# Index scores moved from the attention phase into the last slots of the projections

## The reference, cut to what matters

```python
h = split_columns(x @ w_in)                  # all projections of the mixer
q_idx = apply_rope(q_idx.reshape(B, S, 8, 32), cos_i, sin_i)
k_idx = apply_rope(k_idx, cos_i, sin_i)      # one key of 32 for 8 query heads
rel = relu(einsum('bqhd,bsd->bqhs', qi, k_idx))
score = einsum('bqh,bqhs->bqs', wi, rel)     # 8 heads, weighted by token features
score = where(k_pos <= q_pos, score, -1e30)
_, idx = top_k(score, 128)
```

## Time and profile before

| | |
|---|---|
| median of 3 runs | 3699.91 us (3674.93, 3700.03, 3699.91) |
| the profiled execution | 3671.68 us, of which the span is 3669.9 us |
| granted TensorE clock, mean of the span | 0.964 |
| PE busy / PEld / DVE / ACT | 94% / 75% / 46% / 39% |
| projections, layer 0 (from the first product to the last) | 402.2 to 544.4 us |
| index scores, layer 0 | 553.9 to 571.1 us |
| attention units, layer 0 | to 728.1 us |

### The profile page before, as it was taken

One profiled execution on the slowest core, in us unless ns is written; L12 is line 12 of the kernel. 1 busy time (PEld: TensorE's weight loads), 2 busy tenths in 40 slices (PEclk: granted clock), 3 DMA queues, 4 the chain that ended last, 5 costly groups with the idle time before them and its releaser, 6 DMA issues. The chain is left out here.

```text
span 3669.9 us, 43503 instructions
## 1 busy us (share of the span) xinstructions
PE 3457.0 (94%) x15978; PEld 2748.0 (75%) x15978; DVE 1674.2 (46%) x2929; ACT 1424.3 (39%) x2341; POOL 77.5 (2%) x52
## 2 busy tenths in 40 slices
PE   7999989999999999999998999979999899889998
PEld 5888667677888788777776788757777677768886
DVE  3333448635333433334773533346655437343333
ACT  4332325454332433242545433235544427333321
POOL 0001000010001000100000100100000000000000
PEclk9999998989999999999898999989999999999999
DMA  3332330012332233233000233211211122223331
GB/s 135 97 105 93 103 87 1 1 35 80 97 108 87 70 97 104 95 96 99 12 1 19 80 97 104 95 45 58 70 65 65 59 92 91 85 69 97 97 108 65
DMA packets 81376, 281.21 MB, mean 77 GB/s; under 512 B 14400, under 2 KB 15936, under 8 KB 80704
## 3 DMA queue, kind: packets, MB, share of 16 engines
q1 hardware_dynamic: 81216, 279.13, 23.7%
HBM read 269.12 MB, written 2.10 MB: 74 GB/s over the span
## 5 line engine op out<-in xcount | busy, mean ns | idle before, releaser
L315 DVE TENSOR_TENSOR wlo<-raw,whi 128x1024 fp32r<-128x1024 f32 (+3 forms) x464 | 609.1, 1313 | 1037.6 <-ACT whi L311 1037.4
L343 PE MATMUL ps<-xh,whi 128*128 128x512 f32 x2320 | 912.8, 393 | 16.2 <-DVE xl L2441 6.3
L344 PE MATMUL ps<-xl,whi 128*128 128x512 f32 x2320 | 906.0, 391 | 0.0
L345 PE MATMUL ps<-xh,wlo 128*128 128x512 f32 x2320 | 905.2, 390 | 0.0
L311 ACT ACTIVATE whi<-raw 128x1024 fp32r<-128x1024 f32 (+3 forms) x464 | 515.3, 1111 | 655.8 <-PE ps L345 612.4
L343 PEld LDWEIGHTS ps<-xh,whi 128*128 128x128 f32 x2320 | 437.8, 189 | 117.4 <-issue 24.7
L344 PEld LDWEIGHTS ps<-xl,whi 128*128 128x128 f32 x2320 | 437.8, 189 | 91.5 <-issue 1.7
L345 PEld LDWEIGHTS ps<-xh,wlo 128*128 128x128 f32 x2320 | 437.5, 189 | 91.8
L343 PE MATMUL ps<-ffn_hh,whi 128*128 128x512 f32 x880 | 346.4, 394 | 11.1 <-DVE ffn_hl L747 11.1
L344 PE MATMUL ps<-ffn_hl,whi 128*128 128x512 f32 x880 | 344.6, 392 | 0.0
L345 PE MATMUL ps<-ffn_hh,wlo 128*128 128x512 f32 x880 | 344.2, 391 | 0.0
(11 more groups left out here) (368 smaller groups left out, 4317.7 us busy)
## 6 DMA issues: line engine op xcount, KB each, us to landing
raw<-in_ffn_up SPq DMA_DIRECT2D x216, 512.0 KB, 3.5
raw<-in_ffn_down SPq DMA_DIRECT2D x80, 704.0 KB, 4.0
raw<-in_ssm_in SPq DMA_DIRECT2D x44, 512.0 KB, 3.5
raw<-in_mix_in SPq DMA_DIRECT2D x32, 512.0 KB, 4.0
raw<-in_lru_in SPq DMA_DIRECT2D x20, 512.0 KB, 3.7
raw<-in_mix_out SPq DMA_DIRECT2D x16, 512.0 KB, 3.5
raw<-in_ssm_out SPq DMA_DIRECT2D x16, 512.0 KB, 3.4
raw<-in_lru_out SPq DMA_DIRECT2D x8, 640.0 KB, 3.8
```

The source lines that it names most:

```text
L315: dve.tensor_tensor(self.core.wlo[:, u % HALF, 0:width], self.core.raw[:, u, 0:width], self.core.whi[:, u % HALF, 0:width].bitcast(F32), A ...
L343: pe.matmul(out, c.whi[:, h, w], xh[:, k0 + k], start=first and k == 0, stop=False)
L344: pe.matmul(out, c.whi[:, h, w], xl[:, k0 + k], start=False, stop=False)
L345: mm = pe.matmul(out, c.wlo[:, h, w], xh[:, k0 + k], start=False, stop=last and k == nk - 1)
```

## The change

- Feature slots are reordered: the index features (`iq`) become slots 5 and 6, the compressed keys slot 4. The token block moves to slots 12 to 15 and into banks 0 to 3. The features of the fourth attention kind (`sq`, `sk`) come last, slots 16 to 19 (`stick_features`).
- The splits and the 24 index scores leave `mixer_attention`. Splits are done on ACT and DVE at slots 9 to 13. The scores go into the last four slots: behind each of the first six groups of 3 product matmuls one index score, six a slot, in PSUM banks 4 to 7. Relu, accumulation and masking follow on ACT and DVE inside the projections.
- The side products stand behind slots 3, 5, 6, 7, 13 and 14, and ACT evacuates each of them at the same slot number as PE computes it.
- SP issues the load of `cmp_w1` before slot 4 instead of behind `x_done`, and the copies of queries and keys earlier or later with their slots. Token copies (L1113) come at slot 15, the sigmoids at the end.

```diff
-    feat = [at[n] for n in "cq ckv dk krope ik nq kc vc ks kw dq iq sq sk".split()]
+    feat = [at[n] for n in "cq ckv dk krope ik kc vc iq nq ks kw dq sq sk".split()]
...
-STORED = (CQ, CQ + 1, CKV, KROPE, NSAQ, NSAQ + 1, KCMP, KSLC, DSAQ, DSAQ + 1, IDXQ, IDXQ + 1, SBQ, SBQ + 1, SBK, SBK + 1)
+STORED = (CQ, CQ + 1, CKV, KROPE, KCMP, IDXQ, IDXQ + 1, NSAQ, NSAQ + 1, KSLC, DSAQ, DSAQ + 1, SBQ, SBQ + 1, SBK, SBK + 1)
+TOK_AT = 12
...
+    rels = [(b, h) for h in range(IDXH) for b in range(1, QB)]
+    per_slot = len(rels) // (slots - TOK_AT - NTOK)
...
+                sp.dma_start(c1[:], d["cmp1"][l].rearrange("p (a j n) -> p a j n", a=2, j=16)).then_inc(ph["c1_in"], 16)
                 load(4)
...
-                beside = {3: lat_sums, 6: queries, 9: keys, 10: values, 12: compress, 14: compressed}
...
+                def stick_features(n):
+
+                    pe.wait_ge(ph["tok_out"], n - TOK_AT - NTOK + 1)
+                    pe.wait_ge(ph["lo_done"], n + 1)
+                    out, s = c.ps[:, n % 4], n % HALF
+                    some = list(rels_of(n))
+                    for t in range(DT):
+                        w = slice(t * P, (t + 1) * P)
+                        pe.matmul(out, c.whi[:, s, w], c.xh[:, t], start=t == 0, stop=False)
+                        pe.matmul(out, c.whi[:, s, w], c.xl[:, t], start=False, stop=False)
+                        mm = pe.matmul(out, c.wlo[:, s, w], c.xh[:, t], start=False, stop=t == DT - 1)
+                        if t == DT - 1:
+                            mm.then_inc(ph["slot_used"], 1)
+                        elif t < len(some):
+                            index_scores(some[t])
+
+                beside = {3: lat_sums, 5: queries, 6: keys, 7: values, 13: compress, 14: compressed}
...
-                beside = {2: squares, 4: roots, 7: queries, 10: keys, 11: values, 13: gelus, 15: compressed}
+                beside = {2: squares, 3: roots, 5: queries, 6: keys, 7: values, 9: lambda: index_hi(0), 10: lambda: index_hi(1),
+                          11: lambda: index_hi(2), 13: gelus, 14: compressed, slots - 1: gates}
...
                 for n in range(slots):
+                    relus(n)
                     act.wait_ge(ph["slot_used"], n + 1)
...
+                    if n == TOK_AT + NTOK - 1:
+                        token_out()
+                    if n == TOK_AT + NTOK:
+                        dve.wait_ge(ph["tok_out"], QB)
+                    accumulate(n)
                     ph.lo(dve, n // 4, n % 4, width(n + 2), last=n >= slots - 4)
-                    if n == 5:
+                    if n == 4:
                         latents()
                     if n - 2 in ROTATED:
                         rope(order.index(n - 2))
...
+                    if n in (9, 10, 11, 14):
+                        rope_query((9, 10, 11, 14).index(n))
+                    if n in (10, 11, 13):
+                        index_lo((10, 11, 13).index(n))
+                    if n == 12:
                         windows()
...
-                pe.wait_ge(ph["lo_done"], n_index)
-                for i in range(len(rels)):
-                    index_scores(i)
-
-                pe.wait_ge(ph["relu_done"], len(rels))
```

More of the change, by code:

```diff
@@ L837, in mixer_front, with rels_of @@
     c2 = c.at("cmp_w2", [64, 192], F32, W + 87 * KB)
-    c1 = c.at("cmp_w1", [P, 2, 16, HD], F32, W + 88 * KB)
+    c1 = c.at("cmp_w1", [P, 2, 16, HD], F32, W + 2 * SBQ * KB)
     ukv = c.at("ukv_w", [P, 2, HEADS * HD], F32, W + 98 * KB)
-    hid = c.at("cmp_hid", [64, 2, NCMP], F32, W + 96 * KB)
+    hid = c.at("cmp_hid", [64, 2, NCMP], F32, W + 87 * KB + 768)
+    rel = c.at("idx_rel", [P, 4, SEQ], F32, W + 54 * KB)
     slots = NFEAT + NTOK
     order = list(ROTATED)
-    width = lambda n: D if n < NFEAT else TOKW
+    in_tok = lambda n: TOK_AT <= n < TOK_AT + NTOK
+    feature = lambda n: n if n < TOK_AT else n - NTOK
+    width = lambda n: TOKW if in_tok(n) else D
+    index = (IDXK, IDXQ, IDXQ + 1)
+    rels = [(b, h) for h in range(IDXH) for b in range(1, QB)]
+    per_slot = len(rels) // (slots - TOK_AT - NTOK)
+    def rels_of(n):
+        at = (n - TOK_AT - NTOK) * per_slot
+        return range(at, at + per_slot) if n >= TOK_AT + NTOK else range(0)
     def halves(lo, hi, dim):
@@ L972, in compressed, with index_scores, token_block @@
                     pe.matmul(c.ps[0:NCMP, 5, 0:HD], hid[:, 1], c2[:, P:P + HD], start=True, stop=True).then_inc(ph["kv_done"], 1)
-                beside = {3: lat_sums, 6: queries, 9: keys, 10: values, 12: compress, 14: compressed}
[L975 to L985, removed]
+                def index_scores(i):
+                    b, h = rels[i]
+                    lo = 32 * (h % 4)
+                    if i >= 4:
+                        pe.wait_ge(ph["relu_done"], i - 3)
+                    q = [x[lo:lo + 32, b * P:(b + 1) * P] for x in m.split[IDXQ + h // 4][:2]]
+                    k = [x[lo:lo + 32, 0:(b + 1) * P] for x in m.split[IDXK][:2]]
+                    out = c.ps[:, 4 + i % 4, 0:(b + 1) * P]
+                    pe.matmul(out, q[0], k[0], start=True, stop=False)
+                    pe.matmul(out, q[0], k[1], start=False, stop=False)
+                    pe.matmul(out, q[1], k[0], start=False, stop=True).then_inc(ph["rel_done"], 1)
+                def token_block(n):
+                    j = n - TOK_AT
                     pe.wait_ge(ph["lo_done"], n + 1)
                     for b in range(QB):
-                        out, at = c.ps[:, 4 + b, 0:TW], slice(b * P, (b + 1) * P)
+                        if j == 0:
+                            pe.wait_ge(ph["bank_free"], 4 + TOK_AT - QB + b + 1)
+                        out, at = c.ps[:, b, 0:TW], slice(b * P, (b + 1) * P)
                         for k in range(DT // NTOK):
@@ L997, in _ @@
                             mm.then_inc(ph["tok_done"], 1)
+                def stick_features(n):
[13 more added lines that the diff above has]
+                beside = {3: lat_sums, 5: queries, 6: keys, 7: values, 13: compress, 14: compressed}
+                apply.pe(pe)
+                pe.wait_ge(ph["bank_free"], 2)
+                ph.products_pair(pe, c.ps[:, 0], c.ps[:, 1], c.xh, c.xl, ph["xl_done"])
+                for n in range(2, slots):
+                    if in_tok(n):
+                        token_block(n)
+                    elif n < TOK_AT:
+                        pe.wait_ge(ph["bank_free"], n + 1)
+                        ph.products(pe, n // 4, n % 4, c.ps[:, n % 4], c.xh, c.xl, 0, DT, True, True)
+                    else:
+                        if n == TOK_AT + NTOK:
+                            pe.wait_ge(ph["ilo_done"], len(index))
+                            pe.wait_ge(ph["cmp_done"], 2)
+                        stick_features(n)
+                    if n in beside:
+                        beside[n]()
             @block.scalar
@@ L1100, in _ @@
                         rope(order.index(n - 2))
[L1101 to L1104, removed]
-                        windows()
[L1106 to L1113, removed]
+                    if n in (9, 10, 11, 14):
+                        rope_query((9, 10, 11, 14).index(n))
+                    if n in (10, 11, 13):
+                        index_lo((10, 11, 13).index(n))
+                    if n == 12:
+                        windows()
+                dve.wait_ge(ph["acc_done"], len(rels))
+                for b in range(1, QB):
+                    own = m.picked[b][:, b * P:(b + 1) * P]
+                    dve.tensor_tensor(own, own, c.k["negd"], ALU.add).then_inc(ph["acc_done"], 1)
         ph.end()
@@ L1165, in mixer_attention @@
     pt = c.at("att_pt", [P, 2, SEQ], F32, A_XH + 6 * KB)
-    rel = c.at("idx_rel", [P, 4, SEQ], F32, A_WORK + 84 * KB)
     sizes = {b: (b + 1) * P for b in range(1, QB)}
[L1168 to L1172, removed]
+    picked, allowed, off = m.picked, {}, A_XL
     for b in range(1, QB):
@@ L1194, in _ @@
             def _(pe):
[L1195 to L1206, removed]
                 def scores(u):
```

141 lines of the change are left out of this document (78 added, 63 removed).

## The result

The changed kernel takes 3699.4 us (median of 20 runs), the kernel before 3674.3 (20 runs, the three shown ahead among them; their median of 3699.9 came from the upper of two groups). The ratio of the times is 1.0075, with a 95% interval of 1.0052 to 1.0099: slower by 0.75%, where I had forecast 0.2% less. The runs of both kernels lie in groups. Before: 14 runs from 3671.6 to 3675.0 and 6 from 3698.9 to 3700.0. After: 1 run at 3674.9, 10 from 3696.2 to 3699.5 and 7 from 3725.4 to 3729.4; the ratio leaves out two more at 3732.2, over 1.5% above the fastest and so counted as slow. The executions profiled take 3671.68 before and 3696.42 after, +24.7.

The account below looks back on a forecast made before the run. The prediction took PE's instruction order to bound the kernel; its terms, 19.6 - 17.2 - 2.6 - 1.5 - 1.7 + 0.7 - 1.0, gave -3.7 us a layer, -7.4 in all, from 3699.9 to 3692.5 us; range 3653 to 3722.

Parts of the forecast that it names:

- What bounds the kernel: Whole kernel: the order of PE's own instructions sets the time, with PE busy for 94% of the span.
- Removed: Start of the attention phase: the index scores leave it, -17.2 us a layer.
- the added columns: Last four projection slots: the scores' columns add 12.4 us a layer, +19.6 together with the changes of rows.
- the price of an excursion: Last four slots: going from 128-row to 32-row work and back costs 0.30 us, x 24 = 7.2 us a layer.
- side products: Projections: earlier copies save 2.6, 1.5 (half clock) and 1.7 us a layer; the wait for windows adds 0.7.
- the gap: Between projections and attention phase: ACT's sigmoids no longer wait for DVE's copies of token banks, -1.0 us a layer.
- The clock behind the gap: Start of the attention phase: units bring the clock back as fast when they follow at once, 0 us; low bound -3.2.
- Rival 1: Start of the attention phase: clock comes back by time, not work; +4.9 us a layer, 3709.7 us; chance 0.12.
- rival 3: Behind the gap: the shorter gap doesn't lower the clock; -4.85 us a layer, 3682.8 us; chance 0.10.
- Rival 2: Last four slots: scores mixed with products fall to half clock; +36 us a layer, 3765 us; chance 0.13.
- rival 4: Mixed projection slots: relus, accumulations or weight splits come late, 2 us a slot; +16 us, 3708 us; chance 0.10.
- the last sentence of the sum: Timed runs: a median sits more likely at the upper of two levels, so 3699.9 - 7.4 = 3692.5 us.

## Why the prediction was wrong

**What bounds the kernel: half right.** PE's order sets the time, and moving PE's work hides none of it. But in units 32 to 47 of the attention PE waits for DVE, and I had read the stretch from 577 to 727 as one, "148.49 of 150 us at 1.00". A finer table has 3.73 of 4 us for 655 to 659 in the kernel before.

**Removed, the added columns, side products, the gap: right in kind.** 17.2 us went. The slots with scores take 562.97 - 518.63 = 44.3 us instead of the 21.8 of four bare slots, +22.5 where I had +19.6; the difference is the price of an excursion, 0.42 us and not 0.30, because I counted the first matmul's late weights on the way in only, and the first product behind a score pays them as well (0.33). This lies inside my bounds. The waits for keys and `cmp_v` went, that for the windows rose to 3.7 (I had 3.0). The dip of the clock behind it, which I had left as it was, grew from 6.8 to 10.3 us (0.50 at 499 to 509), about 1.7 us of loss that the sum has at nothing. The gap shrank by 1.3 (1.0).

**The clock behind the gap: better than the value taken, inside its bounds.** In layer 0 it was back at 574.0 (0.50 at 573 to 574, 0.99 at 574 to 575), 6.1 us behind the first score, where before it had taken 26.8. So from unit 3 on the half clock lasts 2.9 us instead of 6.3. Rival 1 is refuted, and rival 3 too: the clock fell in a gap of 4.9 us.

**Rival 2 is refuted:** the mixed slots run at 1.00. So is rival 4: PE has no wait in them.

**Layer 0 alone came out at -2.1 us** up to the end of its attention phase, where I had -3.7. The terms have the right signs, and the two misses, the excursions and the dip behind the windows, are set off in part by the clock behind the gap. With layer 0's 158.3 us in place of layer 1's 186.0 both layers together are 4.6 us shorter, not 7.4, and no timed run shows even that: the one run without a fall (mean clock 0.968) is at 3674.9, while the lower group of the kernel before has its median at 3673.6. One run is too few to say more.

**The step that failed** is the last sentence of the sum, on the two levels of the timed runs. I took 3675 and 3700 for a property of the measurement, that both kernels share, and carried the median over from one to the other. They were the sign of an event of 25 us within the kernel, a stretch at half clock in the attention units, whose frequency the change could alter, and did: from 6 of 20 runs to 17 of 18, in 7 of them twice. In the sum this is a term that the prediction put at nothing without a reason; in the profiled execution it measured 27.7 us. The forecast of 3692.5 lies near the measured 3699.4, but for a wrong reason: it started from the upper level of the kernel before, which is not its median. Rival 2 looked for a fall of the clock in the slots that were edited; nothing in the prediction asked where else the clock stood near its edge. That PE waits for DVE around unit 44 while the clock still holds was to be read in the trace of before.

**What stays open.** That the change acted through the placement of the units is supported by three edits that touch no unit and change the shares (7 of 12 without a fall after a delay of 1.7 us, 8 of 12 in the upper groups after the earlier copies, 6 of 12 after a delay of the kernel before). That placement matters is so supported, not that it is the whole cause: which placement makes the clock fall wasn't tried, and the one shift of the changed kernel left falls in 5 of 12 runs, where the kernel before has them in about one of six.

## What to carry to other kernels

When the runs of one kernel lie in groups, find the event that separates them before predicting a change: it has a place, a price and a frequency, and any edit ahead of it can alter the frequency. Look for stretches in which TensorE waits a little for another engine at full clock; there one more filling matmul per unit held the clock, and one less cost 68 us. It was free in the ten units around the waits (158.3 us) and cost 2 us a layer in twenty. Small matmuls with fewer rows are best put between full ones in bundles, since each excursion costs about 0.42 us whether it holds one score or three.

## What the runs showed of the hardware

- Attention units that hold the clock at 1.00 don't always bring it back once it is lost: after the fall PE was busy 62.10 of 63 us and the stretch's mean clock was 0.51, while the same units ran at 1.00 in layer 0. It came back at 1926, with the scores of unit 67. In the kernel with one filling it stood at 0.50 from 665 to 700 as well. The first units behind the gap, in the same kernel, had brought it back within 3 us of unit 3's scores.
- Among 32-row matmuls back to back the clock fell once although PE was busy (from 1.00 to 0.50 within the index scores of layer 1 in the kernel before with a delay, 14.31 of 15 us busy at 0.52). Between full products, with half of the time each, it stayed (1.00 for 44 us). So PE's busy share alone doesn't tell whether the clock holds.
- Leaving 128-row work for 32-row work and coming back costs 0.42 us at full clock, against 0.30 that the 64-row rows showed for part of it. The Trainium skill (TensorEngine Tiling, Key Properties) says that a change of the tiling mode drains TensorE and a change of the tile doesn't; the traces agree, with 0.1 us more at each of the four steps around a bundle and, in the kernel before with a delay, the next head's first score, in other 32 rows, starting at 1769.41 while the last score of the head before still runs (to 1770.43).
